# Two pairs of heads' score matmuls issued together, every second round of the attentions

## What is computed

```python
# first stack
x = x + gate * nsa_mixer(h)      # compressed keys, selected keys, window keys: 16 heads each, dim 64
x = x + gate * dilated_mixer(h)  # 16 heads in three groups, joined by their log-sum-exp
x = rms_norm(x)
# second stack, layer 0 and 1
x = layer_norm(a * x + mixer_ab(x)); x = layer_norm(a * x + swiglu(x))   # 8 MLA heads (dim 96), 8 windowed heads with a sink
x = layer_norm(a * x + mixer_cd(x)); x = layer_norm(a * x + swiglu(x))   # 8 forgetting heads (dim 66), 8 chunked heads
```

## Time and profile before

| | us |
|---|---|
| median of three runs | 986.23 |
| span of the profiled execution | 984.6 |
| PE busy in it | 954.9 (97%) |
| DVE busy | 645.7 (66%) |
| ACT busy | 471.4 (48%) |
| POOL busy | 180.9 (18%) |
| `nsa` rounds, from its first score matmul | 108.6 to about 183 |
| `dil` rounds | 303.1 to 334 |
| `ab` rounds | 412.6 to 440.7 |
| `cd` rounds | 733.7 to 761.5 |

### The profile page before, as it was taken

One profiled execution on the slowest core, in us unless ns is written; L12 is line 12 of the kernel. 1 busy time (PEld: TensorE's weight loads), 2 busy tenths in 40 slices (PEclk: granted clock), 3 DMA queues, 4 the chain that ended last, 5 costly groups with the idle time before them and its releaser, 6 DMA issues.

```text
span 984.6 us, 15103 instructions
## 1 busy us (share of the span) xinstructions
PE 954.9 (97%) x5656; PEld 806.3 (82%) x5656; DVE 645.7 (66%) x1164; ACT 471.4 (48%) x734; POOL 180.9 (18%) x154
## 2 busy tenths in 40 slices
PE   5999999999999999999999999999999999999996
PEld 2799666878886789988888888879999888888884
DVE  3656567975755775667766766676445776766665
ACT  1453577545445635573344444444457334444442
POOL 2015337204961301230000000010023000000001
PEclk9999999999999999999999999999999999999998
DMA  9865655435564255223465555534532336555541
GB/s 374 352 245 169 235 194 195 149 128 183 201 228 178 89 186 228 87 87 129 154 261 203 209 208 187 187 143 158 190 129 86 129 137 257 187 188 184 187 182 43
DMA packets 24105, 178.37 MB, mean 181 GB/s; under 512 B 3792, under 2 KB 4224, under 8 KB 7928
## 3 DMA queue, kind: packets, MB, share of 16 engines
q1 hardware_dynamic: 19840, 166.70, 45.4%
q0 software_dynamic: 2224, 8.94, 2.9%
q10 hardware_dynamic: 1991, 2.07, 0.8%
HBM read 176.65 MB, written 1.05 MB: 180 GB/s over the span
## 4 chain that ended last, share of the span: by engine, by line
PE 85%; DVE 9%; ACT 2%; DMA 2%; issue 1%; POOL 0%; SPq 0%; DVEq 0%; ACTq 0%; POOLq 0%
PE G L1109 12%; PE G L1111 12%; PE G L1110 12%; PE S L1229 8%; PE T L1229 8%; PE S L1228 4%; PE T L1228 3%; PE T L622 2%; PE T L527 2%; PE G L1309 2%; PE G L1298 2%; PE G L1290 2%; PE G L632 1%; PE G L631 1%; PE G L630 1%; DVE wlo L2174 1%
## 5 line engine op out<-in xcount | busy, mean ns | idle before, releaser
L2312 DVE TENSOR_TENSOR wlo<-ring,whi 128x2048 fp32r<-128x2048 f32 x88 | 154.4, 1758 | 88.4 <-ACT whi L1873 54.0
L1109 PE MATMUL G<-whi,hTh 128*128 128x308 f32 (+3 forms) x480 | 163.9, 341 | 0.5 <-DVE hTl L568 0.3
L1111 PE MATMUL G<-whi,hTl 128*128 128x308 f32 (+3 forms) x480 | 161.1, 336 | 0.0
L1110 PE MATMUL G<-wlo,hTh 128*128 128x308 f32 (+3 forms) x480 | 161.0, 336 | 0.0
L2174 DVE TENSOR_TENSOR wlo<-ring,whi 128x1024 fp32r<-128x1024 f32 (+3 forms) x66 | 105.4, 1635 | 64.9 <-ACT whi L1731 64.7
L1229 PE MATMUL S<-hT,whi 128*128 128x512 f32 x336 | 122.0, 397 | 0.0
L1229 PE MATMUL T<-hT,whi 128*128 128x512 f32 x336 | 120.6, 394 | 0.0
L1109 PEld LDWEIGHTS G<-whi,hTh 128*128 128x128 f32 x480 | 90.2, 188 | 11.2 <-DVE hTl L568 2.4
L1731 ACT CAST whi<-ring 128x1024 fp32r<-128x1024 f32 (+3 forms) x66 | 75.2, 1186 | 44.6 <-PE G L1111 30.1
L1868 ACT CAST whi<-ring 128x2048 fp32r<-128x2048 f32 x44 | 83.9, 1906 | 25.9 <-PE S L1332 17.5
L1110 PEld LDWEIGHTS G<-wlo,hTh 128*128 128x128 f32 x480 | 90.4, 188 | 5.7 <-issue 0.7
(11 more groups left out here) (387 smaller groups left out, 1883.6 us busy)
## 6 DMA issues: line engine op xcount, KB each, us to landing
ring<-in_ffn SPq DMA_DIRECT2D x44, 1536.0 KB, 6.4
ring<-in_dil_w_in SPq DMA_DIRECT2D x16, 1024.0 KB, 4.8
ring<-in_cd_w_in SPq DMA_DIRECT2D x10, 1232.0 KB, 5.4
ring<-in_ada_w SPq DMA_DIRECT2D x12, 1024.0 KB, 6.6
early<-in_ada_w SPq DMA_DIRECT2D x8, 1024.0 KB, 10.1
ring<-in_nsa_w_in SPq DMA_DIRECT2D x5, 1432.0 KB, 7.4
ring<-in_ab_w_in SPq DMA_DIRECT2D x4, 1440.0 KB, 6.4
vec<-in_vecs POOLq DMA_DIRECT2D x11, 512.0 KB, 5.4
```

Of the source, the lines that this page charges most:

```text
L1109: pe.matmul(out_, act_h, w_h, start=first_, stop=False)
L1110: pe.matmul(out_, act_h, w_l, start=False, stop=False)
L1111: return pe.matmul(out_, act_l, w_h, start=False, stop=last_)
L2312: TT(wlo[b][:, part], ring[:, b, part], whi[b][:, part].bitcast(F32), ALU.subtract).then_inc(st[what + "_lo"], 1)
```

## The change

- PE: round p no longer issues scores(p). Rounds 0 and 1 issue their own; round 2 issues scores(2) and scores(3); each later odd round issues scores(p + 1) and scores(p + 2) if these exist; even rounds from 4 on issue none. Turns and products keep their rounds.
- DVE: rounds 0 to 2 do maxima(p); round 2 also does maxima(3), behind its hook; later rounds do maxima(p + 1). The hook that stood after each head's maxima is called twice in a row after them.
- ACT: rounds 0 and 1 do exps(p); from round 1 on a round does copies(p - 1), then exps(p + 1). The hook after each head's exps is called twice in a row behind them.

```diff
+        def scored_in(p, pairs):
+            if p < 2:
+                return (p,)
+            if p == 2:
+                return (2, 3)
+            return (p + 1, p + 2) if p % 2 == 1 and p + 2 < pairs else ()
...
+            def scores(p):
+                if p >= 2:
+                    pe.wait_ge(att["maxes"], 2 * (b0 + 2 * (p - 1)))
+                two = [(jobs[2 * p + e][0], jobs[2 * p + e][1], SB[p % 2][e]) for e in range(2)]
...
             for p in range(pairs + 2):
-                if p < pairs:
...
+                for ahead in scored_in(p, pairs):
+                    scores(ahead)
                 if mid is not None:
                     mid(p)
...
-            for p in range(n // 2 + 2):
+            def maxes(p):
...
+            for p in range(n // 2 + 2):
+                if p <= 2:
+                    maxes(p)
+                elif p + 1 < n // 2:
+                    maxes(p + 1)
+                if between is not None:
+                    between(2 * p)
+                    between(2 * p + 1)
+                if p == 2:
+                    maxes(3)
                 if p >= 2:
                     dve.wait_ge(att["pv"], b0 + 2 * p - 2)
...
             for p in range(n // 2 + 1):
-                if p == n // 2 - 1:
+                if p < 2:
+                    exps(p)
+                if p >= 1:
                     copies(p)
...
+                    if p + 1 < n // 2:
+                        exps(p + 1)
+                if between is not None and p < n // 2:
+                    between(2 * p)
+                    between(2 * p + 1)
                 if p >= 1:
-                    if p != n // 2 - 1:
-                        copies(p)
                     if sink(2 * p - 2):
```

More of the change, by code:

```diff
@@ L632, in times_v @@
                 pe.matmul(o[:, 1, :], pt[:, 2 * P:SW], v[1], start=False, stop=True).then_inc(att["pv"], 1)
-            for p in range(pairs + 2):
-                if p < pairs:
[L636 to L643, removed]
+            def scores(p):
+                if p >= 2:
+                    pe.wait_ge(att["maxes"], 2 * (b0 + 2 * (p - 1)))
+                two = [(jobs[2 * p + e][0], jobs[2 * p + e][1], SB[p % 2][e]) for e in range(2)]
+                for q, k, bank in two:
+                    pe.matmul(bank[:, 0:P], q[:, 0:P], k[:, 0:P], start=True, stop=True)
+                for q, k, bank in two:
+                    pe.matmul(bank[:, P:SW], q[:, P:T], k[:, 0:T], start=True, stop=True).then_inc(att["scores"], 1)
+            for p in range(pairs + 2):
+                for ahead in scored_in(p, pairs):
+                    scores(ahead)
                 if mid is not None:
@@ new lines, in maxes @@
+                    dve.wait_ge(att["scores"], b0 + i + 1)
+                    if i >= 4:
+                        dve.wait_ge(att["turns"], b0 + i - 3)
+                    s, bank, bias, h = scr[:, i % 4, :], SB[p % 2][i % 2], bias_of(i), i % H
+                    if i >= H:
+                        dve.wait_ge(att["probs"], 2 * (b0 + i - H) + 2)
+                    least, scale = 3e38, scale_of(i)
+                    if sink is not None and sink(i) is not None:
+                        least = sink(i)
@@ new lines, in maxes @@
+                    tl.mark(dve.tensor_tensor_reduce(s[:, 1:1 + P], bank[:, 0:P], bias[:, 0:P], -scale, least, ALU.add, ALU.min,
+                                                     negmax[:, h, 0:1]), att["maxes"])
+                    tl.mark(dve.tensor_tensor_reduce(s[:, 1 + P:1 + SW], bank[:, P:SW], bias[:, P:SW], -scale, least, ALU.add, ALU.min,
+                                                     negmax[:, h, 1:2]), att["maxes"])
+                if sink is not None and sink(2 * p) is not None:
@@ L718, in copies, with exps @@
                     act_.copy(probT[:, j % 4, :], TB[j % 2][:, 0:SW]).then_inc(att["turned"], 1)
+            def exps(p):
+                for i in (2 * p, 2 * p + 1):
+                    act_.wait_ge(att["maxes"], 2 * (b0 + i) + 2)
+                    h, s = i % H, scr[:, i % 4, :]
+                    act_.activation(s[:, 1:1 + P], s[:, 1:1 + P], ACT.Exp, bias=negmax[:, h, 0:1], scale=-1.0).then_inc(att["probs"], 1)
+                    act_.activation(s[:, 1 + P:1 + SW], s[:, 1 + P:1 + SW], ACT.Exp, bias=negmax[:, h, 1:2],
+                                    scale=-1.0).then_inc(att["probs"], 1)
             for p in range(n // 2 + 1):
-                if p == n // 2 - 1:
+                if p < 2:
+                    exps(p)
+                if p >= 1:
                     copies(p)
[L723 to L731, removed]
+                    if p + 1 < n // 2:
[3 more added lines that the diff above has]
+                    between(2 * p + 1)
                 if p >= 1:
-                    if p != n // 2 - 1:
-                        copies(p)
                     if sink(2 * p - 2):
```

## The result

The changed kernel took 993.98 us (median of 6 executions, 989.36 to 995.65), the kernel before 986.25 us in the same session; the ratio is 1.0069, 95% interval 1.0052 to 1.0087. It is slower by 7.7 us, where 983.8 us had been forecast and 988.4 was the upper end.

The account below looks back on a forecast made before the run. PE, busy for 954.9 of 984.6 us, bounds the kernel. Terms -1.6 (nsa), -0.15 (dil), -0.4 (ab), -0.25 (cd) sum to -2.4: 982.2 us profiled, 983.8 us median; range 981.0 to 988.4 for 8 in 10.

Parts of the forecast that it names:

- the clock is granted in full in both: In cd and nsa of the kernel before, TensorE's granted clock was read as 1.00, the 2.4 GHz level.
- What one merge is worth: Double rounds of 64-row pairs: second pair's scores cost 0.65 us instead of 0.86, gaining 0.35 us for each merge.
- Rivals 1: Merged rounds: switches are not saved, a second pair costs 0.86 us; 986.1 us, chance 0.17.
- 3 (not issued together): Merged rounds: the second pair's scores wait for the maxima of the pair two back; about 986 us, chance 0.06.
- The cover of the take: Rounds without scores: only turns (0.66 us) cover the take, so products start 0.14 late in cd, 0.46 ab, 0.58 dil.
- the restart: Rounds where products wait for the take: 0.05 us added for each restart of PE.
- Rival 2: Takes don't hold the rounds without scores in dil, ab, cd and nsa; 980.0 us, chance 0.10.
- `ab`: -0.4 forecast: ab: gain of 0.4 us, with 0.3 of scores(3) in a PE wait for ACT and round 7 0.46 late.
- with their longer operands and the sink's addition, at 1.6: ab, round 6: maxima ahead of the take on DVE last 1.6 us, making products 0.46 late in round 7.
- `nsa`: -1.6 forecast: nsa: three times -0.66 us for two rounds, +0.9 at round 8, -1.1 at round 14, -0.5 at the tail.
- 0.9 at round 8: nsa: +0.9 us at round 8, from a delayed compressed branch on DVE and ACT and a longer round 7.
- Rival 4: nsa: ACT's copy out of G3 stands behind exps and near parts, so compressed pieces wait; 4.8 us back, 988.6 us, chance 0.17.

Follow-up runs that it names:

- filled kernel: Changed kernel plus five unread 128x128 identity products before each of nsa's three long waits and ab's: 989.32 us, ratio 1.0028 to the kernel before.
- best kernel: Changed order in nsa, ab, cd, old in dil; nsa's three steps moved, sink addition behind the take, alternating banks in nsa's end, ab, cd: 982.72 us, ratio 0.9973.
- banks without the order: Kernel before, its order kept, with products on alternating banks alone (ab and cd from first pair, dil from pair 4, nsa from pair 12): 985.95 us, ratio 1.0002.
- 994.0 us profile: Profiled execution of the changed kernel run again unchanged; that run's median was 992.68 us, ratio 1.0071.

## Why the prediction was wrong

**The step that failed: "the clock is granted in full in both".** I read the granted clock of the kernel before as a property of the stages and costed every wait at its length. A wait of 1.4 us in the new order cost up to 2.8 us more in clock (`nsa`, 76.52 us against 73.70 filled). This is about half of the 7.7 us: the filled kernel stands at 989.3 us, the changed one at 992.7 when run again, and the stages in which the two profiles of the changed kernel show the 1.2 GHz level, for 6.8 and 13.7 us, are 2.8 and 6.0 us longer than the filled kernel's. No rival had a fall of the clock as its mechanism.

**What one merge is worth.** Right in its mechanism and, for `cd`, in its size: 0.65 us for the second pair, 0.35 us for each double round, once nothing waits. Rivals 1 (0.86 for a second pair) and 3 (not issued together) are refuted by the chain at 147.28 to 148.79. In `nsa` only 0.11 of the 0.35 reached the end, and what held back the rest was not measured; in `ab` nothing did. Of ten double rounds at 0.35 us each, 3.5 us, 1.3 us were real in the best kernel by its stages.

**The cover of the take.** The mechanism was right, and the waits stand in rounds 4, 6 and 7 as said. The chain in `cd`:

```profile
750.41 0.24 PE G L640 x2
750.65 0.02 issue
750.67 0.19 DVE rden L2268
750.86 0.02 issue
750.89 0.43 DVE tok L2270
751.32 0.04 issue
751.36 0.44 PE G L638 x2
```

The mis-sized term is the restart. From the end of one pair's products to the start of the next ones pass 0.71 us where the turns alone take 0.66. That is 0.05 late, less than my 0.14; but the first product of a pair takes 0.44 us behind such a wait and 0.17 without one, 0.27 us where I had put 0.05. In `cd` that is three times 0.32 instead of 0.19, 0.4 us of the 0.5 between the +0.27 measured and the -0.25 forecast. In `dil` PE waits 0.51 us (I said 0.58) and the restart is 0.27 again, three times 0.15 more than forecast: that is half of what lies between +0.71 and -0.15, and the other half I did not place. Rival 2 (the takes hold nothing) is refuted by the same lines.

**`ab`: -0.4 forecast, +1.84 measured.** The failed step is the term "with their longer operands and the sink's addition, at 1.6". From the first maxima of pair 4 (425.94) to the end of the addition (429.00) it took 3.06 us; with the addition at its median of 0.16 us it would have been 1.6. It struck in round 4, where the forecast had the 0.14 us of `cd`, and not in round 6. (By its own terms the forecast for `ab` comes nearer to -0.25 than to -0.4: `cd`'s -0.25, less 0.3 for the wait, plus 0.32 for round 7.) I had read a spread of 0.16 to 1.26 us for the other small DVE instruction with two inputs in SBUF, and had allowed for it in `nsa` alone. Here the new order put such an instruction under POOL's 2.36 us and the take behind it. The run with the addition behind the take gave back 1.6 us. The Trainium skill, "SBUF — State Buffer", section "SBUF: two separate sides", says that a DVE instruction with two SBUF inputs is shut out until a GpSimd instruction that reads SBUF, and that started first, has ended. The ends at 428.98 and 429.00 us agree with it, and so do those of the thirteen other profiles, though no run here changed POOL's instruction to test it.

**`nsa`: -1.6 forecast, +2.95 measured.** With the same waits and no fall it was +0.13 (73.70 us in the filled kernel). With its three waits moved away the stage gained 1.43 us, so the sum was nearly right for a kernel without them. The forecast priced each of the three places too low: round 4's late sum at nothing (it counts it as cover), the first compressed piece within "0.9 at round 8" for the delays ahead, and the tail as a gain of 0.5. Each was in fact a wait of about 1.4 us on a step that stood behind something else in DVE's or ACT's program order: the late sum behind the maxima of the pair ahead, ACT's copy behind that pair's exponentials and two near parts, the take behind POOL's quarter. A double round takes 8.79 us, not 8.55: the turns behind two pairs take 0.81 instead of 0.71, and the compressed piece itself 1.13. DVE's split (L2671), put at 183.8, starts here:

```profile
186.08 1.23 DVE L2671 TENSOR_TENSOR out_lo<-ring,whi 128x1024 fp32r<-128x1024 f32 x1
```

That is 0.66 us later than in the earlier trace rows although `nsa` began 1.2 us earlier.

**Rival 4**, the slower one, had ACT's order as its mechanism. The first compressed piece did wait, 1.43 us, and the run that moved it took the wait away (ACT's copy for it ends at 135.99 us, 0.10 ahead of the piece); the three others waited 0.02 us (153.64), so its 4.8 us were not there. The kernel was slower by other waits of the same kind, and by the clock.

**What stays open.** Not every such wait was followed by a fall. The fourteen profiles have 25 waits of 1.25 us or more within the attentions, and 12 falls; three of the four waits in the changed kernel's own first profile (1.45, 1.43 and 1.69 us) have none behind them. The same kernel's 1.45 and 1.69 us waits did have one in its second profile. What decides between them I did not separate. Of the 3.2 us that the new order cost in `dil`, `ab` and `cd`, 0.7 were not found in the stages.

## What to carry to other kernels

Before a change that makes rounds uneven, list for each round without cover what the waiting engine waits for, through the whole program order of the engine that it waits for, not only the step itself; the costly waits here were on steps that stood behind something unrelated. Price each wait of TensorE twice, once by its length and once by the clock that may fall behind it, and put that as a rival with its own chance. Where a bank's reuse makes the wait, a second bank cures it (6.4 us here, with the falls behind the waits) and is free where nothing waits.

## What the hardware showed that was not expected

In every profile the granted clock was at one of two levels, 1.2 or 2.4 GHz. Within the attentions it fell twelve times in seven profiles, for 3.4 or 6.8 us each time, and every fall began inside a wait of TensorE of at least 1.38 us or at most 2.4 us behind the end of one. The three profiles without such a wait (before, filled, banks without the order) have no fall there. Every profile has one more at the end of its span, where TensorE has no work left (from 977.8 us on before). Just ahead of a fall, TensorE had been busy for 6.60 of 8.00 us (121 to 129 us, 994.0 us profile) or 4.47 of 6.00 (170 to 176 us, changed kernel). With 1.0 us of useless matmuls in each such wait none of seven executions had a clock under 0.996. The Trainium skill, "TensorE: Matmul & The Clock Gate", section "Why this matters for your kernels", gives keeping TensorE free of idle gaps between bursts of matmuls as the way to avoid drops in the middle of a kernel, and the filled kernel bears that out. The gaps that the page warns of are longer than the 1.38 to 1.68 us behind which falls were seen in the new order; there the measurements decide.
